# GpSimd's subtraction for the weights' low parts, cut into four operations

## The reference

```
h = rms_norm(x, g_pre_mix) * (1 + scale1) + shift1        # scale, shift, gate: silu(c) @ w_ada + b_ada (adaLN)
proj = h @ w_in                                           # one projection, columns split among:
  m_qk (2048), m_v (1024), m_o (1024), m_if (8)           #   mLSTM branch: conv + silu, matrix memory
  d_q, d_k (1024 each), d_v (1024)                        #   differential attention branch
  g_m, g_d (1024 each)                                    #   merge gates
merged = sigmoid(g_m) * (y_m @ w_br_m) + sigmoid(g_d) * (y_d @ w_br_d)
x = x + gate1 * rms_norm(merged @ w_out, g_post_mix)
# second sub-layer: product-key retrieval over 16384 single-neuron experts
```

## Time and profile before

| | |
|---|---|
| median of 3 runs | 2004.93 us (2002.63 to 2009.47) |
| profiled execution: its own time | 2008.27 us |
| its span in the trace | 2006.5 us |
| TensorE busy | 1936.8 us (97%) |
| VectorE busy | 1503.3 us (75%) |
| ScalarE busy | 718.4 us (36%) |
| GpSimd busy | 459.2 us (23%), of which L481 138.4 and L484 18.4 us |
| mean granted TensorE clock | 0.99 |

### The profile page before, as it was taken

One profiled execution on the slowest core, in us unless ns is written; L12 is line 12 of the kernel. 1 busy time (PEld: TensorE's weight loads), 2 busy tenths in 40 slices (PEclk: granted clock), 3 DMA queues, 4 the chain that ended last, 5 costly groups with the idle time before them and its releaser, 6 DMA issues.

```text
span 2006.5 us, 27908 instructions
## 1 busy us (share of the span) xinstructions
PE 1936.8 (97%) x10341; PEld 1713.6 (85%) x10341; DVE 1503.3 (75%) x2742; ACT 718.4 (36%) x1327; POOL 459.2 (23%) x235
## 2 busy tenths in 40 slices
PE   5999999999999989999999999999999999999998
PEld 3889777789877878899999999999988888888886
DVE  5677645364476536787889999997689898889885
ACT  4110233010352243343443444444444444444443
POOL 0443210434102123101011511111222223223221
PEclk9999999999999999999999999999999999999999
DMA  6335410454212422257767688888999999999993
GB/s 254 105 105 177 138 63 21 142 173 147 63 43 84 147 85 85 84 171 257 231 227 259 214 325 299 296 303 301 413 384 401 402 400 400 401 401 402 397 368 120
DMA packets 212642, 465.92 MB, mean 232 GB/s; under 512 B 15624, under 2 KB 157120, under 8 KB 193344
## 3 DMA queue, kind: packets, MB, share of 16 engines
q1 hardware_dynamic: 194112, 330.47, 47.3%
q0 software_dynamic: 18432, 134.23, 16.9%
HBM read 410.12 MB, written 54.53 MB: 232 GB/s over the span
## 4 chain that ended last, share of the span: by engine, by line
PE 42%; DMA 8%; DVE 5%; ACT 1%; SPq 1%; issue 1%; POOLq 0%; POOL 0%; DVEq 0%; ACTq 0%
PE xin_ps_u L2075 22%; PE xin_out L2119 16%; DMA experts_hot<-act_scratch 6%; PE xin_out L2097 4%; DMA con_raw<-in_expert_u 2%; DVE over_v_vlo L2386 1%; SPq L2047 1%; DVE in_ulo L2237 1%; DVE experts_rows L1868 1%; DVE experts_acc L1887 1%; DVE xin_wt L2383 1%; ACT in_uhi L2148 0%; DVE xin_wlo L2388 0%; ACT L2190 0%; DVE over_s_stage L2251 0%
## 5 line engine op out<-in xcount | busy, mean ns | idle before, releaser
L1861 POOL DMA_INDIRECT experts_rows<-in_expert_rows,experts_idx x128 | 234.4, 1831 | 886.9 <-DVE experts_acc L1887 752.0
L2075 PE MATMUL xin_ps_u<-con_h_hi,in_uhi 128*128 128x384 f32 x1024 | 348.4, 340 | 10.3 <-DVE in_ulo L2237 8.1
L2075 PE MATMUL xin_ps_u<-con_h_lo,in_uhi 128*128 128x384 f32 x1024 | 342.9, 335 | 0.0
L2075 PE MATMUL xin_ps_u<-con_h_hi,in_ulo 128*128 128x384 f32 x1024 | 342.8, 335 | 0.0
L2119 PE MATMUL xin_out<-over_v_vhi,xin_whi 128*128 128x512 f32 x768 | 238.8, 389 | 2.5 <-DVE xin_wlo L2388 2.4
L2119 PE MATMUL xin_out<-over_v_vlo,xin_whi 128*128 128x512 f32 x768 | 238.4, 389 | 0.0
L2119 PE MATMUL xin_out<-over_v_vhi,xin_wlo 128*128 128x512 f32 x768 | 238.3, 389 | 0.0
L2237 DVE TENSOR_TENSOR in_ulo<-con_raw,in_uhi 128x1024 fp32r<-128x1024 f32 x127 | 155.4, 1223 | 79.0 <-ACT in_uhi L2148 75.2
L2075 PEld LDWEIGHTS xin_ps_u<-con_h_hi,in_uhi 128*128 128x128 f32 x1024 | 192.9, 188 | 14.5 <-DVE in_ulo L2237 11.9
L2075 PEld LDWEIGHTS xin_ps_u<-con_h_lo,in_uhi 128*128 128x128 f32 x1024 | 192.9, 188 | 0.0
L2075 PEld LDWEIGHTS xin_ps_u<-con_h_hi,in_ulo 128*128 128x128 f32 x1024 | 192.6, 188 | 0.0
(11 more groups left out here) (420 smaller groups left out, 3754.3 us busy)
## 6 DMA issues: line engine op xcount, KB each, us to landing
con_raw<-in_expert_u SPq DMA_DIRECT2D x128, 512.0 KB, 5.8
con_raw<-in_expert_v SPq DMA_DIRECT2D x128, 512.0 KB
con_raw<-in_w_in SPq DMA_DIRECT2D x36, 1024.0 KB, 5.8
act_scratch<-in_act SPq DMA_DIRECT2D x128, 192.0 KB
experts_hot<-act_scratch SPq DMA_DIRECT2D x128, 192.0 KB
gate_scratch<-in_stage SPq DMA_DIRECT2D x12, 1024.0 KB
gate_scratch<-over_s_stage SPq DMA_DIRECT2D x12, 1024.0 KB
experts_hot<-gate_scratch SPq DMA_DIRECT2D x16, 768.0 KB
```

The lines of the kernel that those rows point to most:

```text
L1861: pool.indirect_dma_start(out=self.rows[:, r % ROWS, :], out_offset=None, in_=table, in_offset=at).then_inc(self.row_in[r % ROWS], 16)
L2075: mm = pe.matmul(ps_u[s % 2][:, 0:TD], a[s % 2][:, k, :], m[:, k, P:T], start=(i == 0), stop=(i == 3 * KD - 1))
```

## The change

The one operation on 128 x 2048 elements becomes four on 128 x 512 (two of the eight k each), issued one behind the other; only the last increments `w_lo`, so all that waits for the low part waits for the last. It is made at both places, L481 and L484. Nothing else is changed.

```diff
+        def low_part(pool, s):
+            for k in range(0, KD, 2):
+                part = slice(k, k + 2)
+                op = pool.tensor_tensor(wlo[s][:, part], raw[s][:, part], as_f32(whi[s][:, part]), ALU.subtract)
+            op.then_inc(w_lo, 1)
+
         @block.gpsimd
         def _(pool):
...
                         pool.wait_ge(w_hi, gb + 2 * it + s + 1 - before)
-                        pool.tensor_tensor(wlo[s][:], raw[s][:], as_f32(whi[s][:]), ALU.subtract).then_inc(w_lo, 1)
+                        low_part(pool, s)
             if following:
                 pool.wait_ge(w_hi, g0 + 1 - before)
-                pool.tensor_tensor(wlo[0][:], raw[0][:], as_f32(whi[0][:]), ALU.subtract).then_inc(w_lo, 1)
+                low_part(pool, 0)
```

## The result

The changed kernel takes 2010.2 us (median of 20 runs, 2007.3 to 2017.7) against 2004.9 us (20 runs, 2002.6 to 2011.7). The ratio is 1.002, with a 95% interval of 1.0011 to 1.003: slower by 0.2%, 2.2 to 6.0 us. The medians lie 5.3 us apart, the means of the two sets of 20 runs 4.3 us (2010.6 against 2006.3). That is not over the 0.3% that the prediction set as the line of "the same", and 2010.2 us is inside its range of 2001.5 to 2012. But its sum of +1.2 us lies under the measured interval, and the median is 0.1 us above 2010.1 us, the worst that it gave for its own mechanism. The profiled execution has a span of 2008.3 us and an own time of 2010.07 us, 1.8 us over that of before.

A forecast was written before the change was run, and what follows sets the result against it. TensorE, busy 1936.8 of 2006.5 us, bounds the kernel; the edit acts through its waits. The terms -0.5 - 1.7 + 0.15 + 1.55 + 1.7 sum to +1.2 us, moving the median from 2004.93 to 2006.1 us, range 2001.5 to 2012.

The forecast's parts named there:

- its own mechanism: GpSimd and VectorE alternate at the port and pieces are cheap: chance 0.72, range 2003.7 to 2010.1 us.
- (e): Granted clock after TensorE's idles: half-clock stretch probably lost in proj_m (-1.7 us), one probably gained in branch_d (+1.7 us).
- Alternation: At the SBUF port, GpSimd and VectorE take turns: piece, VectorE operation, piece; several L138s over 1 us per N group.
- rivals 1 and 2: GpSimd keeps the port through its pieces: 2005.4 us, chance 0.13; VectorE keeps it for its chain: about 2004.3, 0.05.
- The price of a piece: Each 512-column GpSimd subtraction likely takes 1.15 to 1.2 us; 0.05 us per further start, +0.15 us per group.
- Rival 3: A piece costs 1.64 us, so TensorE waits in seven proj_m T groups: 14.4 us slower, 2019.3 us, chance 0.10.
- (a): proj_m's T groups: +0.15 us per subtraction against 1.0 us of slack, so cost 0.
- (b): proj_m's first N group: VectorE's adaLN chain ends 0.5 us earlier, TensorE idles 1.1 us in place of 1.60.
- (c): proj_d's first group: TensorE's wait for the adaLN chain grows by 0.15 us (-0.2 to +0.3).
- (d): branch_d: GpSimd's subtraction ends 1.55 us later, TensorE idles 2.9 us in place of 1.37.

The follow-up runs named there:

- experiment 3: Changed kernel, with VectorE in branch_d waiting for the low part ahead of its sum of two SBUF operands; ratio 1.0006 to the kernel before.
- experiment 10: Eight operations of 256 columns in branch_d alone, one elsewhere as before; one execution, 2016.0 us against 2009.8 for one of the kernel before.
- experiment 8: Sixteen operations of 128 columns in proj_m alone, one of 2048 elsewhere; ratio 1.002 to the kernel before.
- experiment 2: Four operations in proj_m, branch_m and proj_d, one of 2048 columns kept in branch_d; ratio 1.0006 to the kernel before.
- experiment 6: Changed kernel, with VectorE's weight cast in branch_d made one group earlier; ratio 1.0005 to the kernel before.
- Experiments 1: Four operations in branch_d alone, one of 2048 columns kept elsewhere; ratio 1.0022 to the kernel before.
- experiment 4: The changed kernel measured again, on the same chip as the other follow-up runs; ratio 1.003 to the kernel before.
- experiment 7: Kernel before, one operation of 2048 columns, with VectorE's weight cast in branch_d made earlier; ratio 1.0015 to the kernel before.

## Why the prediction was right, point by point

**The total.** The range held, and in part by luck: the worst case of its own mechanism ended at 2010.1 us, and it was the allowance for the scatter of three runs that took it to 2012. The waits were right. The clock, which its sum put at nothing (-1.7 and +1.7), is the term that was mis-sized, as shown under (e) and below it.

**Alternation** (right; its rivals 1 and 2 fall). While pieces are left, each L138 waits for one piece and the next piece for that L138. The same holds in branch_d, and experiment 3 takes it away by taking VectorE's operations away.

**The price of a piece** (mis-sized). The sum had 0.05 us for each further start; 4 and 16 pieces give 0.14 ((5.04 - 4.61)/3 and (6.73 - 4.61)/15), and 8 pieces 0.13 ((5.55 - 4.61)/7, in the second group of experiment 10, whose pieces ran undisturbed). Rival 3's 1.64 us for a piece is out: alone it is 1.28. Its cost in T groups was also counted wrongly, since a wait is paid in every second group, not in seven (experiment 8; for four dearer pieces that is argued from it, not run).

**(a)** right: no wait, 0.6 us of slack left of 1.0. **(b)** right: 1.02 us of idle against 1.1, and the half clock at 151 us gone in all five traces with four pieces in proj_m, while it stands in all six that keep one piece there. **(c)** right: +0.1 us. **(d)** right in its total, 2.84 us of idle against 2.9, by luck: two errors cancel. The pieces' own growth is 0.43 us and not 0.15, and the three VectorE operations take 1.05 us of the port and not 1.4.

**(e), the term that was mis-sized.** The saving of 1.7 us at (b) was booked as kept. Most traces show it given back 100 us later: in four of the five with proj_m cut in four, the half clock in the mLSTM block lasts 6.8 us in place of 3.4, and experiment 2 loses 1.6 us there. Without that saving the prediction's own sum is -0.5 + 0.15 + 1.55 + 1.7 = +2.9 us. From the traces it is -0.6 + 0.1 + 1.5 + 1.7 = +2.7 us. Both lie within the measured 2.2 to 6.0 us. Why the stretch in the mLSTM block is longer is not shown. TensorE reaches the block 2.4 us earlier in experiment 2 and 2.1 us earlier in experiment 6, but there the stretch was not longer. Nor was it in experiment 8, which has no half clock at (b) either. No run has the cut in proj_m with the clock held, so that the one causes the other is argued from these traces and not shown.

**Where the rest of the loss is.** Experiments 1 and 2 add up to +0.28% and the changed kernel gave +0.2 and +0.3%, so the parts account for the whole. But the centre of these, 4 to 6 us, is above the 2.7 us of the account, and in experiment 4 (2.8 to 9.3 us) the interval only just misses it. A trace has one execution. The span and the mean granted clock are on record for every run but those of before in the first comparison, and an estimate of the time at half clock follows from them, 2 x (1 - clock) x span. The clock has three digits there, a step of 4 us in one run, which evens out over many. The 95% interval is that of the mean:

| kernel | runs | mean span, us | at half clock, us | span less half of that, us |
|---|---|---|---|---|
| before (beside 1 to 4) | 35 | 2004.7 | 31.4 +- 1.6 | 1989.0 +- 0.4 |
| before (beside 5 to 8) | 29 | 2005.0 | 31.8 +- 1.4 | 1989.1 +- 0.4 |
| changed | 20 | 2008.8 | 40.2 +- 2.1 | 1988.7 +- 0.7 |
| changed (4) | 12 | 2010.7 | 42.6 +- 4.8 | 1989.4 +- 0.9 |
| cut in branch_d alone (1) | 12 | 2009.0 | 39.8 +- 2.3 | 1989.0 +- 1.1 |
| all but branch_d (2) | 12 | 2006.0 | 33.8 +- 2.7 | 1989.1 +- 0.8 |
| VectorE held (3) | 12 | 2006.9 | 34.8 +- 3.6 | 1989.5 +- 0.5 |
| changed, early cast (6) | 11 | 2005.3 | 36.8 +- 3.4 | 1986.9 +- 0.6 |
| before, early cast (7) | 11 | 2007.8 | 36.5 +- 2.3 | 1989.6 +- 1.0 |
| sixteen in proj_m (8) | 12 | 2008.1 | 34.5 +- 4.0 | 1990.9 +- 1.0 |

The last column takes half clock under an idle TensorE as lost too, so it parts the two only roughly. Even so, the changed kernel has 9 to 11 us more at half clock than before, two or three stretches of 3.4 us and not the one of the account, and by this estimate that is its whole loss of 4 to 6 us. With the cut in branch_d alone it is the same. The two traces of the kernel before have 39.1 and 27.7 us at half clock within their spans, around a mean of 31; the prediction was worked out on the first, which has more of it than the mean, and that is also why the first pair of traces differs by 1.8 us only (the changed kernel's has 37.0 us, less than its mean). Which stretches are the added ones stays open: those at 322, 336, 674 and 1394 us come and go between executions of one kernel, and no kernel was traced often enough to count them.

No version beat the kernel before. The nearest are experiments 2, 3 and 6, level with it. Experiment 6 has the shortest time outside the half clock (1986.9 us), 2 us under before, and loses them again at half clock.

## What to carry to other kernels

Before an operation is cut so that another engine can get in, ask which of the two is late. The port passes to the waiting engine at each cut, so the cut engine's result is late by every operation let in plus 0.14 us per cut. In these runs that pays where the waiting engine is the late one ((b), experiment 7's VectorE) and costs where the cut one is (branch_d). Price a stall on TensorE with the clock behind it, but don't book a saved half-clock stretch until the next stretches have been looked at, and compare the granted clock of all runs of both kernels before you trust one trace of each.

## What the hardware showed that was not expected

The length of an idle does not tell by itself whether half clock follows. At (b), (c) and (d) the granted clock fell to 0.50 with idles of 1.60, 1.78, 1.94, 2.84 and 4.47 us and stayed at 1.00 with 0.98 to 1.45 us. But TensorE's idle of 1.71 us at some 661 to 670 us, in 11 of the 12 traces, was followed by full clock up to its next long idle in all of them, as was that of 2.16 us in experiment 7. The idle of 2.7 us at 672 us was met by half clock in the first trace of the kernel before, from 673.8 us on, and not in the second:

```profile
671.86 1.13 PE L1376 MATMUL fin_ps_row<-fin_diag,con_ones 128*128 128x128 f32 x8 [2.71 <-ACT fin_row_a L1438]
...
671.90:680.00 8.10, 8.10 (x68) 8.10 (x69) 5.43 (x6) 3.54 (x8) 0.00 (x0) 1.00 0.99 362
```

GpSimd's back-to-back operations of 512 columns take 1.28 us each, start to start 1.25, so a further start costs 0.14 us even with nothing to wait for. Sixteen pieces alternating with a chain of seven make that chain faster than one piece does: at (b) TensorE did not wait for it at all, while GpSimd took 8.07 us there.
